# A second level of seven products in the MLP's down-projection, with the weights' sums made once and kept in HBM

## What is computed

```python
h = rms_norm(x, norm_mlp[i]) * (1 + sc_f) + sh_f
x = x + g_f * (jnp.square(jax.nn.relu(h @ w_mlp_in[i])) @ w_mlp_out[i])
```

## Time and profile before

| | us |
|---|---|
| median of three runs | 2737.46 (2729.74 to 2741.19) |
| span of the profiled execution (no other time is given for it) | 2738.8 |
| PE busy | 2622.4 (96%) |
| DVE busy | 1644.3 (60%) |
| up-projection, first and second half | 740 to 937, 1130 to 1323 |
| down passes, two and two | 937 to 1130, 1323 to 1522 |

### The profile page before, as it was taken

How to read it: one execution, slowest core, us unless ns; L and a number is a source line. 1 busy time by engine, 2 the same in 40 slices (tenths; PEclk the granted TensorE clock), 3 DMA queues, 4 the chain that set the end, 5 groups by cost and what they waited for, 6 DMA issues and landing times. The chain is left out here.

```text
span 2738.8 us, 54602 instructions
## 1 busy us (share of the span) xinstructions
PE 2622.4 (96%) x21658; PEld 1743.5 (64%) x21658; DVE 1644.3 (60%) x4376; ACT 755.8 (28%) x1845; POOL 305.7 (11%) x411
## 2 busy tenths in 40 slices
PE   6999989999999999999999989999999899999996
PEld 4888856664588744688544467777777656444443
DVE  5444268786556557665557358888888667322225
ACT  3211056661310000000000246666666400100002
POOL 0000033310000000000000001111111100643312
PEclk9999999999999999999999999999999999999998
DMA  6010035331022355222445411100000031799995
GB/s 248 32 62 32 1 132 175 126 101 54 16 93 77 142 181 196 81 93 79 168 157 210 158 63 29 29 3 29 29 12 21 18 127 69 257 395 399 398 368 207
DMA packets 108800, 347.02 MB, mean 127 GB/s; under 512 B 8832, under 2 KB 18560, under 8 KB 99472
## 3 DMA queue, kind: packets, MB, share of 16 engines
q1 hardware_dynamic: 100304, 319.01, 32.0%
q0 software_dynamic: 8256, 24.65, 2.4%
HBM read 310.53 MB, written 33.10 MB: 125 GB/s over the span
## 5 line engine op out<-in xcount | busy, mean ns | idle before, releaser
L2078 PE MATMUL mixing_ps<-all_main,pre_ws 64*64 64x256 f32 x3072 | 247.5, 379 | 0.3 <-issue 0.2
L1318 PE MATMUL mlp_ps<-mlp_w2s,all_main 128*128 128x512 f32 x512 | 239.6, 592 | 0.0
L3165 PE MATMUL ex_ps<-all_main,ex_xT 128*128 128x512 f32 x496 | 224.8, 596 | 2.1 <-DVE ex_xT L3323 2.1
L1318 PE MATMUL mlp_ps<-all_main 128*128 128x512 f32 x384 | 183.2, 592 | 0.7 <-DVE all_main L1541 0.7
L1318 PEld LDWEIGHTS mlp_ps<-mlp_w2s,all_main 128*128 128x128 f32 x512 | 96.6, 190 | 117.8 <-issue 105.6
L3165 PEld LDWEIGHTS ex_ps<-all_main,ex_xT 128*128 128x128 f32 x496 | 92.3, 191 | 107.4 <-issue 103.0
L2078 PEld LDWEIGHTS mixing_ps<-all_main,pre_ws 64*64 64x64 f32 x3072 | 134.1, 134 | 19.7 <-issue 1.1
L254 PE MATMUL qkv_ps<-qkv_wq,h_hT 128*128 128x256 f32 x576 | 134.0, 385 | 2.9 <-DVE h_hT L547 2.9
L1318 PEld LDWEIGHTS mlp_ps<-all_main 128*128 128x128 f32 x384 | 72.7, 190 | 93.3 <-issue 70.2
L254 PEld LDWEIGHTS qkv_ps<-qkv_wq,h_hT 128*128 128x128 f32 x576 | 111.2, 193 | 19.6 <-issue 4.1
L1532 DVE TENSOR_TENSOR all_main<-mlp_w2s 128x512 f32<-128x512 f32 x64 | 44.3, 692 | 130.8 <-PE mlp_ps L1318 129.3
(11 more groups left out here) (500 smaller groups left out, 5115.2 us busy)
## 6 DMA issues: line engine op xcount, KB each, us to landing
mlp_w2s<-in_w SPq DMA_DIRECT2D x64, 1024.0 KB, 5.0
all_main<-in_w_gu SPq DMA_DIRECT2D x31, 2048.0 KB, 16.0
all_early<-in_w SPq DMA_DIRECT2D x32, 1024.0 KB, 4.8
att_wa<-in_w_ada SPq DMA_DIRECT2D x32, 512.0 KB, 4.2
all_early<-in_w_d SPq DMA_DIRECT2D x16, 1024.0 KB, 14.3
all_main<-in_w_d SPq DMA_DIRECT2D x16, 1024.0 KB, 14.5
y_rows<-ex_y SPq DMA_DIRECT2D x32, 512.0 KB
qkv_wq<-in_w_qkv SPq DMA_DIRECT2D x6, 2048.0 KB, 8.4
```

Of the source, the lines that this page charges most:

```text
L1318: last = nc.tensor.matmul(ps[:, PRODUCTS.index(name), :], lhsT=lhsT, rhs=rhs, start=j == 0, stop=j == FPAIRS - 1)
L2078: last = nc.tensor.matmul(ps[heads(m), banks[half], 0:UT], lhsT=ws[heads(half), n, k, heads(m)], rhs=columns(k, heads(half)), start=(k == ...
L3165: last = nc.tensor.matmul(pg[:, n % 2, :], lhsT=(xT[:, n % 2, :] if x is None else x)[:, k * P:(k + 1) * P], rhs=gu[n][:, k, :], start=(k ...
```

## The change

The down-projection is made by two levels of the method. The outer level splits tokens, hidden tiles and output columns in two again, so that each half of the tokens (512) takes seven outer products, each of them an inner seven: 14 passes (`PASSES = 2 * HALF_PASSES`), each over 8 quads of hidden tiles and 7 products of 256 columns. Both up-projection halves now run one after the other, and the passes after them.

The weights' sums of both levels don't depend on the tokens. They are made once, during the up-projection, in 16 steps s (`sub_sums`): SP loads 1 MB of `w2`, laid out by sub-blocks on the host, into the memory of `xres`; DVE makes 4 sums of 4 x 128 columns and 4 of 7 x 128 between the adds of the gather; SP stores the 7 x 7 blocks but those that fall out, 128 rows x 7 x 896 values, to `t_rows` in HBM. `xres` is parked in HBM meanwhile (`x_rows`) and comes back before the passes. In a pass SP loads a quad's sums (1792 values a row) through a ring of four. The hidden values of the second half go to HBM (`hid_rows`) and are loaded into `main` after the first half's passes have read it. DVE makes the inner sums of the hidden values in two batches a pass (`inner_sums`) and, for the four outer products that need them, the outer ones (`side_sums`). The squares stay on DVE; their inputs now have a buffer each (`corner`). The residual's turns move to the last pass, two after a quad; `w_head` is loaded into `main`.

SP's program during the up-projection, and what it calls:

```diff
+        def made_from(s):
+            return 18 + 49 * s // 4
+        sub_steps = {made_from(s) + n: (s, n) for s in range(SUBS) for n in range(4)}
+        sub_stores = {made_from(s) + 5: s for s in range(SUBS)}
+        sub_loads = {made_from(s - 1) + 8 if s else 10: s for s in range(SUBS)}
...
+                def sub_load(s):
+                    if s:
+                        sp.wait_ge(sub_out, 16 * s)
+                    else:
+                        sp.wait_ge(parked, 16 * TT)
+                    sp.dma_start(sub_all[:, 0:3, 0:4, :], w2[s // 2, s % 2, :, 0:3]).then_inc(sub_in, 16)
+                    sp.dma_start(sub_12, w2[s // 2, s % 2, :, 3]).then_inc(sub_in, 16)
+                def sub_store(s):
+                    sp.wait_ge(sub_made, 8 * s + 8)
+                    sp.dma_start(t_rows[:, s // 2, :, s % 2, :].rearrange("o p n -> p o n"),
+                                 sub_all[:, :, 1:8, :].rearrange("p o i n -> p o (i n)")).then_inc(sub_out, 16)
...
+                sp.wait_ge(xn_done, TT)
+                for t in range(TT):
+                    sp.dma_start(x_rows[t * P:(t + 1) * P, :], xres[:, t, :]).then_inc(parked, 16)
+                for n in range(2 * FPAIRS):
+                    if 1 <= n < 2 * FPAIRS - 1:
+                        pair_weights(n + 1)
+                    for i in range(7):
+                        at = 7 * n + i
+                        if at in sub_stores:
+                            sub_store(sub_stores[at])
+                        if at in sub_loads:
+                            sub_load(sub_loads[at])
+                        if i == 3 and n > FPAIRS:
+                            hidden_store(n - 1)
+                        if at == made_from(SUBS - 1) + 6:
+                            sp.wait_ge(sub_out, 16 * SUBS)
+                            for t in range(TT):
+                                sp.dma_start(xres[:, t, :], x_rows[t * P:(t + 1) * P, :]).then_inc(x_back, 16)
```

`pair_weights(n)` still waits until the products and sums of pair n - 2 are done. DVE's part (in `gather(n, j)` a call `between(i)` stands ahead of u2 for i = 0 and behind u2, u3, u4, c22 for i = 1 to 4; i = 5 stands between the first two squares, i = 6 behind c21):

```diff
+                    def between(i):
+                        if 7 * n + i in sub_steps:
+                            sub_sums(*sub_steps[7 * n + i])
...
+                    if n == 0:
+                        dve.wait_ge(sub_in, 32 * s + 32)
+                        if s:
+                            dve.wait_ge(sub_out, 16 * s)
+                        nc.vector.tensor_tensor(outer[0], sub_12, b11, ALU.subtract).then_inc(sub_made, 1)
+                        nc.vector.tensor_tensor(outer[2], b22, sub_12, ALU.subtract).then_inc(sub_made, 1)
...
+                    if n == 3:
+                        dve.wait_ge(sub_made, base + 5)
+                        nc.vector.tensor_tensor(within[1], x22, within[0], ALU.subtract).then_inc(sub_made, 1)
+                        dve.wait_ge(sub_made, base + 7)
+                        nc.vector.tensor_tensor(within[3], x21, within[1], ALU.subtract).then_inc(sub_made, 1)
```

The order of DVE in the stage, and a product of the down passes:

```diff
+                        if n + 1 < 2 * FPAIRS:
+                            every(sums_of(n + 1))
+                        else:
+                            inner_sums(0, 0)
+                        gather(n, j, next_tokens if n == FPAIRS - 1 else iter(()))
+                for g in range(PASSES):
+                    inner_sums(g, 1)
+                    if g:
+                        finish(g - 1)
+                    if g + 1 < PASSES:
+                        if OUTER[(g + 1) % HALF_PASSES] in ("m5", "m6", "m7", "m3"):
+                            side_sums(g + 1)
+                        inner_sums(g + 1, 0)
...
+                    place = IN_PLACE[name]
+                    rhs = ring[n % RING][:, 0:14 * P].rearrange("p (c i t) -> p i c t", c=2, i=7)[:, place]
+                    last = nc.tensor.matmul(ps[:, PRODUCTS.index(name), 0:QB].rearrange("p (c t) -> p c t", c=2), lhsT=lhsT, rhs=rhs,
+                                            start=j == 0, stop=j == QUADS - 1)
...
+                        if g == PASSES - 1:
+                            turn_residual(2 * j - 4)
+                            turn_residual(2 * j - 3)
```

More of the change, by code:

```diff
@@ L989, in step @@
         ins.then_inc(ended, 1)
[L990 to L999, removed]
+        return done[0]
     copied(2)
     at2 = step(nc.vector.tensor_tensor(m6, m6, m1, ALU.add))
-    yield
@@ L1004, in finish_pass @@
-    copied(3)
+    copied(4)
+    at11 = step(nc.vector.tensor_tensor(m1, m1, m2, ALU.add))
     dve.wait_ge(ended, at2)
     at3 = step(nc.vector.tensor_tensor(m7, m7, m6, ALU.add))
-    yield
     at4 = step(nc.vector.tensor_tensor(m6, m6, m5, ALU.add))
-    yield
     dve.wait_ge(ended, at3)
[L1011 to L1021, removed]
+    step(nc.vector.tensor_tensor(m5, m5, m7, ALU.add))
     copied(6)
+    step(nc.vector.tensor_tensor(m4, m4, m7, ALU.add))
     dve.wait_ge(ended, at4)
[L1024 to L1029, removed]
+    whole = step(nc.vector.tensor_tensor(m3, m3, m6, ALU.add))
@@ new lines, in finish_pass @@
+    targets = TARGETS[name]
+    halves = sorted({half for _, half in targets})
+    rows_of = C["rows"].rearrange("p (t c) -> p t c", t=2)
+    temp_of = temp.rearrange("p (t c) -> p t c", t=2) if temp is not None else None
+    for n, half in enumerate(halves):
+        cs = slice(half * NB, (half + 1) * NB)
+        out = rows_of if n == len(halves) - 1 else temp_of
+        dve.wait_ge(ended, whole)
+        scaled = step(nc.vector.tensor_tensor(out, rows_of, gate[:, cs].unsqueeze(1).to_broadcast([P, 2, NB]), ALU.mult))
+        dve.wait_ge(ended, scaled)
+        for side, to in targets:
+            if to == half:
+                xs = xres[:, t0 + 2 * side:t0 + 2 * side + 2, cs]
+                step(nc.vector.tensor_tensor(xs, xs, out, ALU.add))
@@ L1159, in _, with pair_weights @@
             def _(sp):
[L1160 to L1163, removed]
+                def pair_weights(n):
                     if n == 1:
@@ L1168, in pair_weights @@
                         sp.wait_ge(summed, 4 * (n - 1))
[L1169 to L1179, removed]
+                    sp.dma_start(w1s[:, n % 2, :, :], w1[n % FPAIRS]).then_inc(w1_in[n % 2], 16)
@@ new lines, in gather @@
+                    corner_free("c22")
+                    add(n, "c22", corner["c22"], "m5", u3)
+                    between(4)
+                    corner_free("c11")
+                    add(n, "c11", corner["c11"], "m2", first_copy)
+                    square("c22", 1, QB)
+                    between(5)
+                    square("c11", 0, 0)
+                    corner_free("c21")
+                    add(n, "c21", corner["c21"], "m4", u3)
+                    next(next_tokens, None)
@@ L1613, in inverse_root @@
                     nc.vector.reciprocal(st[:, 2, hs], st[:, 1, hs]).then_inc(rstd_ok, 1)
-                def some(steps, count):
-                    for _ in range(count):
-                        next(steps, None)
-                def pass_sums(g, between):
-                    for key in made_order(g):
-                        down_sums(g, *key)
-                        if key[0] >= 2 and key[1:] == (3, "S"):
-                            between()
                 out_sum_rows(0, 0)
```

401 lines of the change are left out of this document (240 added, 161 removed).

## The result

The changed kernel takes 2874.7 us (median of 4 runs, 2869.4 to 2882.9) against 2737.5 us for the kernel before on the same chip (2729.7 to 2741.2): ratio 1.051, 95% interval 1.0484 to 1.0537. The forecast was 2856 with a range of 2775 to 2910.

The account below looks back on a forecast made before the run. TensorE bounds the kernel before; the change adds a chain on SP's queue in the up-projection. 2738.8 - 46.3 + 159 + 4 + 1.8 = 2857.3, less 1.3: 2856 us, range 2775 to 2910.

Parts of the forecast that it names:

- The chain of the up-projection: Up-projection: store, load, sums and w1 wait in turn on SP's queue; 15 steps take 454 us against 316, +138 us.
- The kinds: Up-projection step types by first portion's position: 29.7 us at 2, 28.5 at 0, 29.6 at 5, 34.4 at 4.
- the fixed part: Up-projection transfer price: 2.4 us fixed, from 1.05 MB in 4.95 us at 410 GB/s.
- The chain without w1: Rival, up-projection: chain binds but w1 gets through; 25.3 us a step, kernel about 2770 us; chance 0.10.
- The down passes: Down passes: 784 matmuls of 256 columns replace 448 of 512, gaining 46.3 us, with TensorE full.
- The matmul part: Down passes: 256-column matmuls at 0.4316 us each, 338.4 us against 384.7; a pass every 24.2 us.
- nothing waits there, by 1.2 us: Down passes: ring loads land 4.8 us after issue, against a shortest lead of 6.0 us.
- The four second turns of the residual: Last down pass: paired turns share one bank, each second waits about 1.0 us; +4 us in all.
- the 1.8 us for the third load: First down pass: its third load stands behind the last hidden store; +1.8 us.
- the fourth rival: Down passes turn DMA-bound: loads miss the 6.0 us lead, 1 us twice a pass, +28 us, 2885; chance 0.06.
- The clock: Rival, up-projection: TensorE's idle pieces lower its clock; ten long stalls add 28 us, 2884; chance 0.06.

Follow-up runs that it names:

- w1act: Changed kernel with w1 issued by ACT on its own queue instead of by SP: 2814.5 us, ratio 1.0287.
- order10: Changed kernel with each step's sub-block load two products later in SP's order, so w1 can pass ahead of the wait for the store: 2851.5 us, ratio 1.0427.
- raw3: Against `raw2`, all portions of a step's sums made in one gather, and the outer part of the store sent first: 2746.7 us, ratio 1.0041.
- hid: Changed kernel with the hidden values brought back in sixteen 0.52 MB loads instead of two of 4.2 MB: 2873.9 us, ratio 1.0509.
- raw2: Changed kernel with w1 on ACT, split store, hidden values in pieces, and raw blocks alternating between two buffers so loads needn't wait for stores: 2774.1 us.
- split: Changed kernel with each step's store in two DMAs, raw blocks first, the next load waiting for that part only: 2876.1 us, ratio 1.0517.

## Why the prediction was right, step by step

- **The chain of the up-projection** (454 us from the first store's landing to the sixteenth's): measured 1259.80 - 802.86 = 456.9. The stretch before it was 67.1 us, where the forecast's sums leave 67. The kinds, by the issue of the load that waits for the landing: position 2, 29.5 us on average (29.7 forecast); 0, 30.1 (28.5); 5, 28.8 (29.6); 4, 34.6 (34.4). The store lands in 10.0 us at the median of 16 (10.3), w1 in 8.2 (7.6). From the last landing to the down passes: 29.6 us (28.3). Stage: 553.6 against 390.3 + 159 = 549.3. `w1act` shows what w1's place in SP's order is worth, 70 us of the 163, and `order10` gets 33 us by that queue's order alone. `raw3` shows that the sums and the bytes by themselves cost no more than 20 us over before. In the prices one reading is off: the fixed part was taken from a 1.05 MB load in 4.95 us, and the row has 4.8. By the row each transfer would be some 0.15 us shorter and the chain some 4 us, so the close fit of the total holds to a few us only.
- **The chain without w1** was put at 25.3 us a step and the kernel at 2770; `w1act` has 2814.5. That rival's size was too low: a step took 402.7 / 15 = 26.8 us, and VectorE still waited 48.2 us for w1, 81.5 for sub-blocks and 16.0 for the stores of hidden values, a term that the prediction doesn't have.
- **The down passes, where a term was missing.** The matmul part holds: 24.17 us a pass (24.2). The term "nothing waits there, by 1.2 us" fails. It left out the two hidden-value loads of the changed kernel, 4.2 MB each in the middle of the ring's order; three passes' worth of ring loads around them took 1492.85 - 1400.03 = 92.8 us for 72.5, so +20.3: 15.6 of waits, the rest is mostly work at the lower clock. And the ring loads that go to w2's buffers land in 6.3 us against the lead of 6.0, where I took w1's 4.8; TensorE waited six times 0.59 to 0.85 us for ring loads, five of them for w2's buffers, and each such wait made the work about 1 us later: the pass from 1314.75 to 1339.99 took 25.24, +1.07 us for a wait of 0.79. The four second turns of the residual cost 0.85 us each over the 0.43 of a turn (1640.70 - 1639.42 = 1.28), near the 1.0 forecast; the 1.8 us for the third load show nowhere. Together 374.6 us where 391.5 - 46.3 + 5.8 = 351.0 was forecast: the 23.6 us are the largest miss, and of the sign of the fourth rival, but mostly for another cause, a bulk load rather than steady traffic. `hid` bears this out by half: in pieces 9.8 us came back, and the other half stayed with the same bytes.
- **The clock.** It fell to 0.89 over the up-projection and to 0.86 to 0.90 around the two waits of the down passes. In the up-projection TensorE was busy 553.6 - 121.2 = 432 us where 32 pairs at full clock are 387. Most of these 45 us seem not to have lengthened the stage: the steps came out as forecast with no term for the clock, and VectorE waited for TensorE 9.9 us in all. But w1's issue waits for TensorE too, for the pair before, so how much they added stays open. In the down passes, where TensorE is the bound, the clock cost most of the 4.7 us above. The matmuls right behind the waits of 6.65, 8.06 and 7.55 us ran at about half pace, and by that the trace agrees with the Trainium skill's TensorE: Matmul & The Clock Gate (HAM oscillation).
- **The sum.** Forecast for the profiled execution 2857.3, measured 2875.4. The 18.1 us are +4.3 in the up-projection, +23.6 in the down passes, and -9.8 of start and rest, for which nothing in the change accounts. So the up-projection's mechanism was right, and that the total is no further off is in part luck: 9.8 us of scatter hid as much of the down passes' miss.

## What to carry to other kernels

When work moves into a stage with idle engines, price it as a chain on the queue that issues it: each wait in that queue's order is added to the period, whatever share of the DMA engines is idle. Here nearly the same bytes and sums took 554 us with everything in one order on one queue and in one buffer, and 410 with w1 on a second queue, a second buffer and another order, and the largest single repair was to take the critical load off the queue with the waits. And where loads are timed to the microsecond, list every other transfer that goes out in that stretch: 4.2 MB ahead of a 0.92 MB load cost waits of 7.6 to 10.0 us here (the changed kernel, `raw2` and `raw3`), and in pieces they cost less only while the rate has room. In every version tried, the saving of 46 us in matmuls was worth less than what the traffic and the sums it brought cost.

## What the runs showed of the hardware

- A 3.2 MB store from 128 partitions landed in 9.3 to 11.2 us. In `split`, where the next load was issued while the store's second part was still under way, that load landed in 8.6 us instead of 4.6.
- A 1 MB load issued by ACT landed in 5.3 us while SP's 3.2 MB stores went on, against 8.2 us from SP. How much of this is the other queue and how much the later place in the traffic was not separated.
- Loads of 0.92 MB, back to back with 0.52 MB pieces, ran at 383 GB/s with the DMA engines at 97%, and TensorE waited: this is where the passes became bound by bytes.
